# Attention's input products in three fp32r passes, with their halves, rotations and compressed softmax reordered

## What is computed

```python
u = rmsnorm(h, kv_norm)
kv = (u @ kv_w).reshape(B, S, 6, 4, 64)               # k_c, v_c, k_s, v_s, k_w, v_w
k_s = rope(rmsnorm(k_s, k_norm[1]), pos)
k_w = rope(rmsnorm(k_w, k_norm[2]), pos)
k_cmp = rope(rmsnorm(compress(k_c, ...), k_norm[0]), cmp_last)
v_cmp = compress(v_c, ...)                            # gelu(blocks @ w1 + b1) @ w2 + b2, 15 blocks
z = rmsnorm(h, norm_g) @ w_in                         # 1024 query columns, 48 gate columns
q = rope(rmsnorm(z[..., :1024], q_norm_g), pos)
gates = sigmoid(z[..., 1024:] + gate_b)
o = gt0 * softmax(q k_cmp) v_cmp + gt1 * softmax(q k_s) v_s + gt2 * softmax(q k_w) v_w
h = h + o @ w_out
```

## Time and profile before

| what | us |
|---|---|
| median of 3 runs | 2324.26 |
| lowest and highest | 2321.26, 2324.26 |
| the profiled execution's own time | 2323.76 |
| its span | 2322.2 |
| busy in the span: TensorE | 2293.6 |
| VectorE | 1694.8 |
| ScalarE | 1378.1 |
| GpSimd | 104.5 |

### The profile page before, as it was taken

One profiled execution on the slowest core, in us unless ns is written; L12 is line 12 of the kernel. 1 busy time (PEld: TensorE's weight loads), 2 busy tenths in 40 slices (PEclk: granted clock), 3 DMA queues, 4 the chain that ended last, 5 costly groups with the idle time before them and its releaser, 6 DMA issues.

```text
span 2322.2 us, 30322 instructions
## 1 busy us (share of the span) xinstructions
PE 2293.6 (99%) x11616; PEld 1902.5 (82%) x11616; DVE 1694.8 (73%) x1617; ACT 1378.1 (59%) x1249; POOL 104.5 (5%) x111
## 2 busy tenths in 40 slices
PE   8999999999999999999999999999999999999998
PEld 7988857988888878888987788888888888888886
DVE  7755545754557776645667788888888888889897
ACT  4643314653356855433568566777777777777775
POOL 0000020000001200000011010000000000000020
PEclk9999999999999999999999999999999999999999
DMA  7555445165625346445343499999999999999993
GB/s 242 182 200 216 145 141 184 62 237 198 217 84 181 109 145 253 176 162 205 118 152 120 147 357 415 417 405 370 388 368 387 369 391 366 392 367 391 367 387 125
DMA packets 205668, 588.55 MB, mean 253 GB/s; under 512 B 9180, under 2 KB 19616, under 8 KB 205584
## 3 DMA queue, kind: packets, MB, share of 16 engines
q1 hardware_dynamic: 198736, 564.28, 65.0%
q0 software_dynamic: 6656, 23.04, 2.6%
q10 hardware_dynamic: 192, 0.05, 0.0%
HBM read 573.19 MB, written 14.16 MB: 253 GB/s over the span
## 4 chain that ended last, share of the span: by engine, by line
PE 96%; DVE 2%; ACT 1%; issue 0%; DMA 0%; DVEq 0%; ACTq 0%
PE ps L1471 9%; PE ps L1470 9%; PE ps L1472 9%; PE ps L811 8%; PE ps L813 8%; PE ps L812 8%; PE ps L1510 4%; PE ps L1509 4%; PE ps L1511 4%; PE ps L689 3%; PE ps L1239 2%; PE ps L1241 2%; PE ps L1240 2%; PE ps L681 2%; PE ps L1173 1%; PE ps L699 1%
## 5 line engine op out<-in xcount | busy, mean ns | idle before, releaser
L2172 DVE TENSOR_TENSOR more_low<-more_parts,high_parts 128x2048 fp32r<-128x2048 f32 x192 | 432.0, 2288 | 33.6 <-ACT high_parts L1578 32.5
L1578 ACT ACTIVATE high_parts<-more_parts 128x2048 fp32r<-128x2048 f32 x192 | 364.6, 1918 | 101.2 <-PE ps L1511 51.8
L1470 PE MATMUL ps<-high_parts,xmh 128*128 128x512 f32 x896 | 352.3, 393 | 0.0
L1472 PE MATMUL ps<-high_parts,xml 128*128 128x512 f32 x896 | 349.1, 390 | 0.0
L2172 DVE TENSOR_TENSOR raw_low<-raw,high_parts 128x2048 fp32r<-128x2048 f32 x144 | 324.0, 2287 | 26.6 <-ACT high_parts L1578 26.6
L1578 ACT ACTIVATE high_parts<-raw 128x2048 fp32r<-128x2048 f32 x144 | 276.0, 1921 | 92.0 <-PE ps L1472 47.5
L1725 ACT ACTIVATE wh<-raw 128x4096 fp32r<-128x4096 f32 (+1 forms) x55 | 189.5, 3446 | 188.1 <-PE ps L813 177.4
L2349 DVE TENSOR_TENSOR wl<-raw,wh 128x4096 fp32r<-128x4096 f32 (+1 forms) x55 | 230.4, 4190 | 70.2 <-ACT wh L1725 70.2
L811 PE MATMUL ps<-wh,xh 128*128 128x512 f32 (+1 forms) x632 | 243.8, 386 | 1.8 <-issue 1.2
L813 PE MATMUL ps<-wh,xl 128*128 128x512 f32 (+1 forms) x632 | 239.6, 379 | 0.0
L812 PE MATMUL ps<-wl,xh 128*128 128x512 f32 (+1 forms) x632 | 239.5, 379 | 0.0
(11 more groups left out here) (555 smaller groups left out, 4327.1 us busy)
## 6 DMA issues: line engine op xcount, KB each, us to landing
more_parts<-in_moe_w_gate SPq DMA_DIRECT2D x78, 1024.0 KB, 5.1
more_parts<-in_moe_w_up SPq DMA_DIRECT2D x66, 1024.0 KB, 7.0
raw<-in_moe_w_down SPq DMA_DIRECT2D x64, 1024.0 KB, 6.8
more_parts<-in_moe_w_down SPq DMA_DIRECT2D x48, 1024.0 KB, 6.1
raw<-in_moe_w_up SPq DMA_DIRECT2D x46, 1024.0 KB, 5.2
raw<-in_w_in SPq DMA_DIRECT2D x22, 2048.0 KB, 8.0
raw<-in_f_w_in SPq DMA_DIRECT2D x20, 2048.0 KB, 8.5
raw<-in_moe_w_gate SPq DMA_DIRECT2D x34, 1024.0 KB, 6.9
```

The costliest lines, as they stand in the source:

```text
L1470: mm(o, xmh[:, k, :], hi[:, cs], start=(k == 0), stop=False)
L1472: t = mm(o, xml[:, k, :], hi[:, cs], start=False, stop=(k == KD - 1))
L1578: fn(part_high(j), part_raw(j), ACT.Copy).then_inc(hi_done, 1)
L2172: v.tensor_tensor(part_low(j), part_raw(j), part_high(j).bitcast(F32), ALU.subtract).then_inc(lo_done, 1)
```

## The change

The input products of attention are made in three fp32r passes. `entry_product` replaces `product` for (`kv`, 0), (`b_in`, 0), (`b_in`, 1) and (`kv`, 1), in two halves of four rows of the contraction; `window_part` and the gate columns get the same passes. The high halves of the weights are ScalarE's (`high_entry`), in buffers that `ENTRY_AFTER` says when to reuse, and the low halves VectorE's (`low_entry`); the token inputs are split in the same manner (`high_tile`, `low_tile_of`) out of the turned rows, which now stay in four banks. The 48 gate columns get a transfer of their own on GpSimd's queue and no slot. The zeros of `zeroed` are written by ScalarE, the rotation tables by GpSimd. Each evicts other products than before: ScalarE takes both token tiles of (`kv`, 1) and (`kv`, 2). The last two key rotations become one over both token tiles (`late_key_phase`). The compressed scores are masked after the first two maxima, their exponential follows step 0's, the weights are normed after the first outputs, and the turned weights lie in steps 3 and 4. The diff, cut to its core:

```diff
-                self.e, self.f = Ring([6], e_filled, e_read), Ring([7], f_filled, f_read)
+                self.e, self.f = Ring([6, 5], e_filled, e_read), Ring([7, 2], f_filled, f_read)
...
-        COMPRESSED_AT = [1, 2]
+        COMPRESSED_AT = [3, 4]
...
+        ENTRY_HIGH = {("kv", 0): (0, 1), ("b_in", 0): (0, 1), ("b_in", 1): (2, 0), ("kv", 1): (1, 2), ("kv", 2): (0, 3)}
+        ENTRY_AFTER = {("b_in", 0, 0): ("kv", 0, 0), ("b_in", 0, 1): ("kv", 0, 1), ("b_in", 1, 1): ("b_in", 0, 0),
+                       ("kv", 1, 0): ("b_in", 0, 1), ("kv", 1, 1): ("b_in", 1, 0), ("kv", 2, 0): ("b_in", 1, 1),
+                       ("kv", 2, 1): ("gates", 0)}
...
+            def entry_product(key, hi_, lo_, tokens=None, between=None, rings=(me.v, me.a)):
...
+                for half in range(2):
+                    me.see(mh_ready)
+                    me.see(ml_ready)
+                    hi, lo = entry_high(key, half), entry_view(key, half, raw_low)
+                    for m, ring in enumerate(rings):
+                        if half == 0:
+                            if tokens:
+                                turned(tokens[m])
+                            banks.append(ring.claim(pe))
+                        o, ms = ps[:, banks[m], :], slice(m * P, (m + 1) * P)
+                        for kk_ in range(4):
+                            k = 4 * half + kk_
+                            mm(o, hi_[:, k, ms], hi[:, kk_, :], start=(k == 0), stop=False)
+                            mm(o, hi_[:, k, ms], lo[:, kk_, :], start=False, stop=False)
+                            t = mm(o, lo_[:, k, ms], hi[:, kk_, :], start=False, stop=(k == KD - 1))
+                        if half:
+                            t.then_inc(ring.filled, 1)
+                        elif m:
+                            t.then_inc(rows_used, 1)
+                            rows_made[0] += 1
+                        if between and half and m == 0:
+                            between()
+                    entry_used[(*key, half)] = (me.a.filled, me.a.n) if half else (rows_used, rows_made[0])
...
+            entry_product(("kv", 0), uh, ul, tokens=(1, 2))
+            entry_product(("b_in", 0), ubh, ubl, tokens=(3, 4))
+            entry_product(("b_in", 1), ubh, ubl)
...
-                product(me.v, ("b_in", 2), m, ubT, w=3 * NH)
-            released(("b_in", 2), me.v)
+                b, ms = me.v.claim(pe), slice(m * P, (m + 1) * P)
+                for k in range(KD):
+                    o = ps[:, b, 0:3 * NH]
+                    mm(o, ubh[:, k, ms], gates_high[:, k, :], start=(k == 0), stop=False)
+                    mm(o, ubh[:, k, ms], gates_low[:, k, :], start=False, stop=False)
...
+            entry_product(("kv", 1), uh, ul, between=hidden_products, rings=(me.a, me.a))
...
-                    t = mm(ps[:, b, 0:256], uT[:, k, m * P:(m + 1) * P], w[:, k, c0:c0 + 256], start=(k == 0), stop=(k == KD - 1))
+                    mm(o, uh[:, k, ms], hi[:, k, :], start=(k == 0), stop=False)
+                    mm(o, uh[:, k, ms], lo[:, k, :], start=False, stop=False)
+                    t = mm(o, ul[:, k, ms], hi[:, k, :], start=False, stop=(k == KD - 1))
...
+            window_part(me.a, 0, 0)
+            window_part(me.a, 1, 0)
...
+            window_part(me.a, 0, 1)
+            turn_keys(0)
+            window_part(me.a, 1, 1)
+            released(("kv", 2), me.a)
+            turn_keys(1)
...
+            def high_entry(key, half):
+                arrived(act, key)
+                if (*key, half) in ENTRY_AFTER:
+                    act.wait_ge(*entry_used[ENTRY_AFTER[(*key, half)]])
+                elif key == ("kv", 0):
+                    act.wait_ge(u_done, FFN_END["ffn0"])
...
+            high_entry(("kv", 0), 0)
+            high_entry(("kv", 0), 1)
+            high_tile(0, uh, "kv_norm")
+            squares(0)
+            high_tile(1, uh, "kv_norm")
+            squares(1)
+            high_tile(0, ubh, "b_norm")
+            square_root()
+            high_entry(("b_in", 0), 0)
+            high_tile(1, ubh, "b_norm")
             fn(ident_r[:], C("ident"), ACT.Copy).then_inc(causal_ready, 1)
             fn(causal_r[:], C("neg_causal"), ACT.Copy).then_inc(causal_ready, 1)
...
+            high_entry(("b_in", 0), 1)
+            high_entry(("b_in", 1), 0)
+            high_entry(("b_in", 1), 1)
+            act.wait_ge(small_in, GATES_IN)
+            fn(gates_high[:], gates_raw[:], ACT.Copy).then_inc(mh_ready, 1)
             queries(0)
             root(NH // 2)
+            fn(zeroed[:], C("one")[:, 0:1].to_broadcast([P, zeroed.shape[1]]), ACT.Copy, scale=0.0).then_inc(zeroed_set, 1)
             root(NH // 2)
...
+            act.wait_ge(q_ready, M)
...
+            high_entry(("kv", 1), 0)
+            high_entry(("kv", 1), 1)
...
+            high_entry(("kv", 2), 0)
+            high_entry(("kv", 2), 1)
+            keys_values(1, 0)
...
+            late_keys(0)
+            late_keys(1)
+            root(M * NG)
+            late_values(0)
             turned_keys(0)
+            late_values(1)
             turned_keys(1)
...
+                if i == 0:
+                    me.see(cdif_ready)
+                    fn(cs[:], cs[:], ACT.Exp, scale=SCALE).then_inc(cexp_ready, 1)
...
+            def low_entry(key, half):
+                me.see(mh_ready)
+                v.tensor_tensor(entry_view(key, half, raw_low), entry_view(key, half), entry_high(key, half).bitcast(F32),
...
+            ffn(0, beside=lambda: low_tile_of(0, uh, ul, "kv_norm"), ahead=lambda: low_entry(("kv", 0), 0))
+            low_tile_of(1, uh, ul, "kv_norm")
+            low_entry(("kv", 0), 1)
+            me.see(norm_sq, M)
+            v.tensor_scalar(small[:, 2:4], small[:, 0:2], 1.0 / D, EPS, ALU.mult, ALU.add).then_inc(norm_ms, 1)
+            low_tile_of(0, ubh, ubl, "b_norm")
+            roots()
...
+            low_tile_of(1, ubh, ubl, "b_norm")
+            low_entry(("b_in", 0), 1)
+            low_entry(("b_in", 1), 0)
+            low_entry(("b_in", 1), 1)
+            me.see(mh_ready)
+            v.tensor_tensor(gates_low[:], gates_raw[:], gates_high[:].bitcast(F32), ALU.subtract).then_inc(ml_ready, 1)
             dve.wait_ge(bc_in, 16 * len(BC))
...
+            dve.wait_ge(pool_filled, TABLES)
...
+                src = kvn[:, :, 768:1024].rearrange("p m (g d) -> p m g d", d=HD)
+                a, b2 = two(tmp_a), two(tmp_b)
+                table = lambda j: rope_k[:, :, 1, j, :].unsqueeze(2).to_broadcast([P, M, NG, HD])
+                link(v.tensor_tensor(a, src, src, ALU.mult))
...
+            for key in (("kv", 1), ("kv", 2)):
+                low_entry(key, 0)
+                low_entry(key, 1)
+            key_phase(0)
...
+            late_key_phase()
...
-            v.tensor_tensor(pcp[:, :, :, 0:NCMP], cs[:], per_head_c, ALU.mult).then_inc(pc_ready, 1)
+            compressed_scores()
             for i in range(1, len(STEPS)):
                 if i + 1 < len(STEPS):
                     maxima(i + 1)
                 outputs(i - 1)
+                if i == 1:
+                    compressed_weights()
...
-            nc.gpsimd.memset(zeroed[:], 0.0).then_inc(zeroed_set, 1)
...
+            def tables(dst, cos, sin, g, rows=P):
+                nc.gpsimd.tensor_tensor(dst[0:rows, 0, :], C(cos, rows), g[0:rows], ALU.mult)
+                return nc.gpsimd.tensor_tensor(dst[0:rows, 1, :], C(sin, rows), g[0:rows], ALU.mult)
+            gq, gk = bc[:, 0:HD], [bc[:, 64 + i * HD:64 + (i + 1) * HD] for i in range(3)]
+            po.wait_ge(const_in, 16)
+            po.wait_ge(bc_in, 16 * len(BC))
+            for m in range(M):
+                tables(rope_g[:, m], f"cos{m}", f"sin{m}", gq)
+                for w in range(2):
+                    tables(rope_k[:, m, w], f"cos{m}", f"sin{m}", gk[1 + w])
+            tables(rope_g[:, 2], "cosc", "sinc", gk[0], NCMP).then_inc(pool_filled, 1)
```

More of the change, by code:

```diff
@@ L215, in weight_plan @@
     tile("kv", 0)
-    for t in range(3):
+    for t in range(2):
         tile("b_in", t)
@@ L250, in build @@
         x = sbuf("x", [P, M, D])
+        with ExitStack() as st:
+            high_x = sbuf("high_x", [P, KD, HW], F32R, stack=st)
         xn = sbuf("xn", [P, M, D])
@@ L936, in _, with turned @@
             ffn("ffn0", (me.e, me.f))
[L939 to L945, removed]
+            def turned(n):
+                for s_ in (e_read, f_read):
+                    pe.wait_ge(s_, n)
+            rows_made = [0]
+            def entry_product(key, hi_, lo_, tokens=None, between=None, rings=(me.v, me.a)):
+                banks = []
+                for half in range(2):
[21 more added lines that the diff above has]
+                    entry_used[(*key, half)] = (me.a.filled, me.a.n) if half else (rows_used, rows_made[0])
+                released(key, me.a)
             def turn_keys(w):
@@ L1025, in _, with hidden_products @@
-            t.then_inc(v_filled, 1)
```

(35 more changed lines are left out.)

269 lines of the change are left out of this document (132 added, 137 removed).

## The result

| | median, us | runs, us | profiled: span, mean granted clock |
|---|---|---|---|
| before | 2324.26 | 2321.26 to 2324.53 (8) | 2322.2, 0.998 |
| after | 2330.35 | 2324.86 to 2334.22 (8) | 2327.6, 0.995 |

The account below looks back on a forecast made before the run. TensorE's own instruction stream was taken as the bound. Up to the scores -9.6 us, softmax +1.3 and clock +0.9 gave -7.4, so 2323.76 became 2316.4 us, range 2312.5 to 2321.5.

Parts of the forecast that it names:

- The products: Key/value and query tiles: 64 products 512 wide fall from 0.858 to 0.68 us each, -11.4 us.
- the wait of 0.9: Start of query tile 0: TensorE, ready at 301.3, waits for VectorE's low half until 302.2, +0.9 us.
- I cost these at nothing ... Room is left.: Work moved off VectorE costs nothing; block reads, issued by 318.51, come in time for TensorE at 324.0.
- The rival about GpSimd's tables: Tables delay the compressed blocks' scratch chain; gain used up at 1.84 us a product; 2341 us at 3.07; chance 0.05.
- Its price stays hidden: Tables on GpSimd, despite contention with VectorE, cost the kernel nothing below 1.3 us a product.
- The clock: TensorE's dip after turnings and gate products stays, plus half the price of another: +0.9 us, bounds -1.7 and +3.4.
- the clock takes more: Gate passes, turnings and new waits bring two more dips than before, +3.4 us: 2318.9 us; chance 0.15.
- the signs that it named as "wrong": Idle before block turnings; half clock 7 us or more; query-tile gaps released by low halves; gate passes far from 0.113.
- The waits at the window tile and the key turning: Fourth window product starts 1.9 us later, behind VectorE's order; both key turnings wait 0.2 and 0.4 us.
- The softmax: VectorE does 1.9 us more inside the steps, so TensorE idles: +1.3 us, bounds 0 and 1.9.
- The gates' term: Sixteen narrow gate products become 48 passes of 0.113 us: +1.4 us; 0.2 a pass would give +5.6.
- -9.6 + 1.3 = -8.3: Forecast without the clock: -9.6 us up to the first attention scores, +1.3 in the softmax.

Follow-up runs that it names:

- e4_tables: The changed kernel with the fourteen rotation-table products back on VectorE and the zero fill back on GpSimd: 2330.1 us, ratio 1.0020.
- e1_hold: The changed kernel with the 2 MB transfer of the first compression weight tile held until the sixteen block reads have landed: 2323.5 us, ratio 0.9990.
- e10_before_slots: The kernel before, with only the gate tile moved out of the weight slots to GpSimd's queue and its own buffer: 2324.2 us, ratio 1.0003.
- e3_soft: The changed kernel with the compressed scores, their exponentials and weights back at their old places in the softmax: 2328.1 us, ratio 1.0014.
- e6_both: The changed kernel with the 2 MB held, gate passes inside query tile 1, compressed scores before the fourth window product, compressed softmax in old places: 2317.7 us, ratio 0.9978.
- e7_late: The changed kernel with the 2 MB held, compressed scores' products before the fourth window product and compressed softmax in its old places: 2320.6 us, ratio 0.9985.
- the last two: e6_both and e11_again, the same kernel measured in two sets: 2317.7 and 2318.1 us.
- e11_again: The same kernel as e6_both, run once more in a later set beside the kernel before: 2318.1 us, ratio 0.9975.
- e2_fill: The changed kernel with 15 added products 512 wide, which nobody reads, in front of TensorE's wait for the compressed blocks: 2326.1 us, ratio 1.0006.
- the three kernels with the wait: The changed kernel, e3_soft and e4_tables, all with the full wait for the compressed blocks: 2330.4, 2328.1 and 2330.1 us.

## Why the prediction was wrong, point by point

**The products: right in kind, small in size.** 48 of them with the wait of 0.9 taken off are 33.94 us, 0.707 each, where 0.68 was taken from a feed-forward stage. 0.03 x 64 = 1.7 us. The wait of 0.9 us at the start of query tile 0 came out in the number, but by luck: e4_tables shows that 0.64 of it is the contention with GpSimd's tables, for which the sum had nothing; the rest of that chain was put about as much too long.

**The step that failed: "I cost these at nothing ... Room is left."** The sum compared when the reads were *issued* (318.5) with when TensorE would want them (324.0) and took "about 2" us for the last landing, which had taken 5.2 even before. It looked at GpSimd's queue, and not at what SyncE's queue would do with the slot that the gate tile no longer filled. In its place the runs show a way through scratch that is 7.4 us longer, where 3.9 us of margin were left: 3.5 us of wait in the profile. Holding the 2 MB back gives 5.5 us of work over all runs. e1_hold and e10_before_slots show both halves of the cause. The rival about GpSimd's tables named the right chain and the wrong reason: 0.3 us a product, far from its break-even of 1.84. "Its price stays hidden" failed too, by 0.6 us: what the tables cost was VectorE's time and not their own.

**The clock: right in kind, seven times too small.** This is the second term that failed. +0.9 was put in, with +3.4 as a bound; over all runs it was +6.7 (1.5 either way), in this stage of the profiles 1.7 before and 10.2 after. The rival "the clock takes more" bounded the number of dips and took each at its old length of 3.4 us. The dips of these kernels are 3.4 to 20.5 us long (the longest in e3_soft). Of the signs that it named as "wrong", two came: idle time in front of the turnings, though not from the tables, and half clock for more than 7 us (331.0 to 344.7). Work at half clock makes the narrow work longer: the 48 gate passes took 0.213 us each at 1.2 GHz, where e6_both ran them at 0.11 at 2.4.

**The waits at the window tile and the key turning:** 1.9 and 0.4 forecast, 1.76 and 0.28 measured; the other turning had none. **The softmax:** two small brackets at the fourth step as forecast, but 0.57 us in the profile, not 1.3; most of the rest of its +4.5 is the second dip (3.4).

**The gates' term** was right at full clock (0.113 forecast, 0.11 in e6_both), and its upper bound of 0.2 a pass is what half clock makes of it.

**The sum again.** Without its term for the clock the forecast for the work is -9.6 + 1.3 = -8.3. Measured, each against the before of its own set (after against that of e1 to e4, the clocks of its own not being on record): -0.9 after, -6.4 with the hold, -7.5 in e7_late, -6.8 and -6.4 in the last two. So the mechanism of the gain was there, 5.5 us of it went with the collision, and the clock took the rest.

**Open:** what decides the place and length of a dip. In ten of the twelve profiles one stands at or behind the turnings and gate passes, in e10_before_slots and e11_again none (e3_soft's begins in the wait in front of the turnings); seven have one between 384 and 417 us, at the window keys or in the first steps of the softmax. TensorE was busy through nearly all of each. That idle time ahead makes the clock take more rests on e1_hold and e2_fill against the three kernels with the wait.

## What to carry to other kernels

When a tile leaves a shared slot plan, walk the loading engine's queue again: the transfer behind it moves up, and ask which small, dependent transfers it will run beside. When a stage is shortened, compare with the *landing* of what it ends on, and take the landing as it will be in the new company. Small, narrow matmuls on the critical path are also a bet on the clock: judge them by the mean clock of many runs, not by one profile. Putting them beside wide ones looks better here, but isn't shown to be. And when work goes to an idle engine, ask what it does to the engine beside it: GpSimd had time for the tables, but they slowed VectorE, and TensorE was waiting for VectorE.

## What the runs showed of the hardware

- A chain of small transfers is slowed by a large one from another queue: the landing of the write of 512 KB went from 3.1 to 7.5 us, that of sixteen reads of 60 KB from 2.4 to 7.0 (medians), with 2 MB transfers beside them. The reads issued before the second 2 MB went out still took 2.4.
- The granted clock fell to 1.2 GHz behind narrow matmuls although TensorE did not idle: in e1_hold it fell just behind 334.2 us, and in the 7.2 us before, the last query products, the turnings and the gate passes kept the engine busy for 7.11 (the row below). The clock differs from run to run, and the runs of one kernel spread over 9 us with it (after: 2324.9 at a mean clock of 0.997, 2334.2 at 0.992).

```profile
327.00:334.20 7.20, 7.11 (x59) 6.47 (x57) 6.13 (x16) 0.90 (x2) 0.00 (x0) 1.00 1.10 349
```

The Trainium skill (TensorE: Matmul & The Clock Gate, Part 1) says that the clock's default is the low level and that the engine's activity releases it. This row does not agree with that as it stands: the clock fell although the profile has the engine busy, and no run here shows why.

- One fp32r pass 48 columns wide took 0.11 us (e6_both, at 2.4 GHz), as one of 128 columns did.
- A GpSimd product of 64 columns beside a VectorE subtraction that reads two SBUF inputs took 2.36 us instead of 0.32, and the subtraction 2.96 instead of 2.28 (after against e4_tables).
